# Sparse attention in a hybrid decoder layer: the top-k mask leaves the score products and is applied to the probabilities by VectorE

## The reference

```python
index = jnp.einsum('bqh,bqhs->bqs', iwb, jax.nn.relu(logits)) * idx_scale
index = jnp.where(causal[None], index.astype(jnp.float32), -jnp.inf)
_, sel = lax.top_k(index, topk)
...
s = jnp.einsum('bqhd,bqkd->bqhk', qb, kg) * scale
p = masked_softmax(s, valid)
return jnp.einsum('bqhk,bqkd->bqhd', p.astype(vg.dtype), vg)
```

## Time and profile before

| | |
|---|---|
| median of the runs | 3528.93 us (3526.89 to 3529.4) |
| profiled execution | 3532.62 us, of which span 3530.8 us |
| busy over the span | TensorE 96%, its weight loads 82%, VectorE 66%, ScalarE 51%, GpSimd 34% |
| mask products in D steps (L1737) | 272, of which 266 for tiles 2 to 15 |

### The profile page before, as it was taken

How to read it: one execution, slowest core, us unless ns; L and a number is a source line. 1 busy time by engine, 2 the same in 40 slices (tenths; PEclk the granted TensorE clock), 3 DMA queues, 4 the chain that set the end, 5 groups by cost and what they waited for, 6 DMA issues and landing times. The chain is left out here.

```text
span 3530.8 us, 55543 instructions
## 1 busy us (share of the span) xinstructions
PE 3376.6 (96%) x18952; PEld 2899.2 (82%) x18952; DVE 2319.4 (66%) x4885; ACT 1805.0 (51%) x3062; POOL 1190.9 (34%) x1963
## 2 busy tenths in 40 slices
PE   6999889899999999999999997999999999999998
PEld 6999777788888888888788785888888788888876
DVE  9899576667777777667743546765645666665364
ACT  4443356677877887886773333333323433333232
POOL 4343244554443333323220234332301435332031
PEclk9999999999999999999999998999999999999999
DMA  4345310000000000000010554322234532332444
GB/s 167 117 165 163 92 33 18 24 20 18 18 18 15 12 18 10 15 7 7 10 41 7 180 159 150 131 72 96 80 130 170 190 99 84 105 110 85 141 142 170
DMA packets 190051, 290.20 MB, mean 82 GB/s; under 512 B 33490, under 2 KB 130002, under 8 KB 189778
## 3 DMA queue, kind: packets, MB, share of 16 engines
q1 hardware_dynamic: 187700, 286.23, 24.5%
q10 hardware_dynamic: 2080, 0.52, 0.1%
HBM read 211.74 MB, written 74.97 MB: 81 GB/s over the span
## 5 line engine op out<-in xcount | busy, mean ns | idle before, releaser
L1849 ACT ACTIVATE shared<-a_ps_st 128x512 f32<-128x512 f32 x716 | 453.1, 637 | 262.3 <-PE a_ps_st L1737 154.3
L2982 PE MATMUL f_ps<-f_x_four,f_w_hi 128*128 128x512 f32 x1408 | 437.4, 392 | 11.8 <-DVE f_w_lo L3120 11.8
L2982 PE MATMUL f_ps<-f_x_three,f_w_hi 128*128 128x512 f32 x1056 | 325.5, 389 | 2.0 <-DVE f_w_lo L3120 2.0
L2982 PEld LDWEIGHTS f_ps<-f_x_four,f_w_hi 128*128 128x128 f32 x1408 | 266.1, 189 | 68.6 <-DVE f_w_lo L3120 13.3
L1761 PEld LDWEIGHTS a_ps_o<-a_vsl,shared 128*128 128x128 f32 x2176 | 289.1, 196 | 19.5
L1761 PEld LDWEIGHTS a_ps_o<-a_dv,shared 128*128 128x128 f32 x2176 | 282.2, 192 | 10.8
L1548 POOL TENSOR_SCALAR a_tk<-a_tk,a_halves 128x1 f32<-128x1 f32 x336 | 105.0, 312 | 539.6 <-ACT a_junk_a L1856 537.2
L1761 PE MATMUL a_ps_o<-a_vsl,shared 128*128 128x65 f32 x2176 | 280.5, 273 | 0.0
L2982 PE MATMUL f_ps<-f_x_four,f_w_lo 128*128 128x512 f32 x704 | 275.3, 391 | 0.0
L1761 PE MATMUL a_ps_o<-a_dv,shared 128*128 128x65 f32 x2176 | 273.8, 269 | 0.0
L3015 PE MATMUL f_ps<-f_w_hi 128*128 128x512 f32 x680 | 265.6, 391 | 4.9 <-DVE f_w_lo L3129 4.8
(11 more groups left out here) (405 smaller groups left out, 8816.9 us busy)
## 6 DMA issues: line engine op xcount, KB each, us to landing
shared<-in_w_down SPq DMA_DIRECT2D x88, 512.0 KB, 3.3
px_raw<-in_x_t SPq DMA_DIRECT2D x48, 512.0 KB, 4.6
shared<-in_w_gate SPq DMA_DIRECT2D x44, 512.0 KB, 5.0
shared<-in_w_up SPq DMA_DIRECT2D x44, 512.0 KB, 4.8
g_scratch<-shared SPq DMA_DIRECT2D x22, 1024.0 KB, 7.5
shared<-g_scratch SPq DMA_DIRECT2D x88, 256.0 KB, 3.5
z_scratch<-p_z SPq DMA_DIRECT2D x16, 768.0 KB, 5.2
o_scratch<-a_oacc SPq DMA_DIRECT2D x32, 256.0 KB, 2.1
```

The lines of the kernel that those rows point to most:

```text
L1849: act.activation(p_t[:, s % PT_RING, :], ps_st[s % ST_BANKS][:, :], ACT.Exp, scale=SCALE).then_inc(exp_done, 1)
L2982: mm = pe.matmul(out[:, :], w[:, j, k * P:(k + 1) * P], x_part(j, x)[:, k], start=(k == 0 and i == 0), stop=(k == 3 and i == 2))
```

## The change

For D quads of tiles 2 to 15 the mask product is no longer part of the score. Each mask is instead transposed once per tile by new side jobs "turn" (one per 512 keys: up to four products of a 128 x 128 piece of `mask_d` with the identity, on TensorE); ScalarE takes exp(0.125 x mask) of it into `keep_d`, which is 1 for a kept key and 0 for a masked one, in int8. After ScalarE's exponential of each D step, VectorE replaces p by min(1e30 x keep, p) in place ("keep" below), and the PV product waits for that. Planner constants change: a turn job costs 50, `MASK_TIME` is -300. The pick of the next mask waits for the last turn of the mask before (instead of the last D score). The scratch `junk_a` becomes int8, and two phases share a semaphore.

```diff
-SIDE_COST = {"max": 550, "cmax": 600, "idx": 680, "prep": 600, "aug": 150}
+SIDE_COST = {"turn": 50, "max": 550, "cmax": 600, "idx": 680, "prep": 600, "aug": 150}
-STEP_TIME, MASK_TIME, LEAST_ROOM = 1500, 0, 0.3
+STEP_TIME, MASK_TIME, LEAST_ROOM = 1500, -300, 0.3
...
+        for t in range(2, TILES):
+            for c in range(self.chunks[t]):
+                r = self.topk_due(t) + c
+                add(r, max(r + 1, self.first("D", t) - 2 * (self.chunks[t] - c)), SIDE_COST["turn"], ("turn", t, c))
...
+    d_steps = [s for s, (n, j) in enumerate(steps) if quads[n][0] == "D" and quads[n][1] >= 2]
+    d_no = {s: b for b, s in enumerate(d_steps)}
...
+        keep_d = sb("a_keep_d", [P, TILES, P], mybir.dt.int8)
-        junk_a = sb("a_junk_a", [P, SEQ], BF16)
+        junk_a = sb("a_junk_a", [P, SEQ], mybir.dt.int8)
...
+            def turn_mask(job):
+                _, t, c = job
+                if c == 0:
+                    pe.wait_ge(mask_d_done, mask_d_value(t))
+                out = side_bank(job)
+                w = min(CHUNK, (t + 1) * P - c * CHUNK)
+                for b in range(w // P):
+                    lo = c * CHUNK + b * P
+                    mm = pe.matmul(out[:, b * P:(b + 1) * P], mask_d[:, lo:lo + P], ident_b[:, :], start=(b == 0), stop=(b == w // P - 1), skip_group_check=True)
+                mm.then_inc(group_turned, 1)
...
-                    if kind == "D":
+                    if kind == "D" and i < 2:
                         pe.wait_ge(mask_d_done, mask_d_value(i))
...
-                    mask = mask_d[:, j * P:(j + 1) * P]
+                    mask = mask_d[:, j * P:(j + 1) * P] if i < 2 else None
...
+                if s in d_no:
+                    pe.wait_ge(kept, d_no[s] + 1)
...
+            def take_mask(job):
+                _, t, c = job
+                w = min(CHUNK, (t + 1) * P - c * CHUNK)
+                act.wait_ge(group_turned, turn_no[job] + 1)
+                if t >= 3 and c == 0:
+                    act.wait_ge(kept, d_no[plan.last[number[("D", t - 1, 1)]]] + 1)
+                dst = keep_d[:, 4 * c:4 * c + w // P, :].rearrange("p b q -> p (b q)")
+                act.activation(dst, ps_side[side_no[job] % SIDE_BANKS][:, 0:w], ACT.Exp, scale=SCALE).then_inc(evac_done, 1)
...
-                    dve.wait_ge(st_done, plan.after("D", t - 1))
+                    if t == 2:
+                        dve.wait_ge(st_done, plan.after("D", t - 1))
+                    else:
+                        dve.wait_ge(group_turned, turn_no[("turn", t - 1, plan.chunks[t - 1] - 1)] + 1)
...
+            def keep(s):
+                n, j = steps[s]
+                p = p_t[:, s % PT_RING, :].rearrange("p (h q) -> p h q", h=4)
+                dve.wait_ge(exp_done, s + 1)
+                if j == 0:
+                    dve.wait_ge(evac_done, evac_no[("turn", quads[n][1], plan.chunks[quads[n][1]] - 1)])
+                dve.scalar_tensor_tensor(p, keep_d[:, j, :].unsqueeze(1).broadcast_to([P, 4, P]), 1e30, p, ALU.mult, ALU.min).then_inc(kept, 1)
...
             for s in range(S + PV_LAG + 1):
+                if s - 1 in d_no:
+                    keep(s - 1)
...
-        fixed_set = sem("m_fixed_set")
+        fixed_set = mixer.fixed_set
...
-        fixed_set = sem("f_fixed_set")
+        fixed_set = mixer.fixed_set
...
-            pool.wait_ge(fixed_set, 3)
+            pool.wait_ge(fixed_set, 6)
```

More of the change, by code:

```diff
@@ L1339, in attention_phase @@
         exp_done = sem("a_exp_done")
+        kept = sem("a_kept")
         pv_done = sem("a_pv_done")
@@ L1771, in side @@
                     prep(job)
+                elif job[0] == "turn":
+                    turn_mask(job)
                 else:
@@ L1862, in evacuate @@
                     take_aug(job[1])
+                elif job[0] == "turn":
+                    take_mask(job)
                 elif job[0] == "idx":
@@ L2569, in __init__ @@
         self.x_lo_done = ctx.enter_context(nc.semaphore("f_x_lo_done"))
+        self.fixed_set = ctx.enter_context(nc.semaphore("f_fixed_set"))
     def part(self, j, low):
```

## The result

The changed kernel takes 3583.96 us (median of four executions, 3578.55 to 3597.02) beside 3528.55 us of the kernel before: a ratio of 1.0159 with a 95% interval of 1.0144 to 1.0174. It is 55 us slower. 3521 us had been predicted, with 3490 to 3556 as the range. The profiled execution took 3580.2 us with a span of 3578.4, so the trace has to explain 47.6 us of span.

A forecast was written before the change was run, and what follows sets the result against it. TensorE's queue was taken as the bound, ScalarE equally full in D g = 0 stages. Terms -13.3 - 3.2 + 0 + 12.5 - 26 + 9 + 13.3 = -7.7 us gave a 3521 us median, range 3490 to 3556.

The forecast's parts named there:

- I cost this at nothing on balance, with the two steps as cover: D steps: PV products waiting for keeps, and keeps for exponentials, cost 0 because VectorE may be two steps behind.
- Product, 0.23 us each: D steps from tile 2 on: 266 mask products leave TensorE at 0.23 us each, 61.2 us in all.
- Turns, 13.3 us: S stages: 133 mask blocks transposed on full TensorE at 0.10 us each cost 13.3 us; ScalarE's 41 evacuations count nothing.
- Keeps, 0.66 us each: VectorE in D steps: 266 added instructions at 0.66 us each, 175 us in all.
- g = 0, nothing, held by ScalarE: D(4..13), g = 0: ScalarE keeps its 189.8 us and VectorE rises to 189.0 of 192.2 us; gain 0.
- g = 1, +12.5 before the planner's part, about nothing with its 1.3 us a stage: D(4..13), g = 1: VectorE, at 226.8 us, exceeds the 202.3 us; 12.5 lost, planner giving back 1.3 a stage.
- The planner, -26 and +9: Side jobs leaving 20 D stages give back 26 us; the 40 or so jobs cost 9 us where TensorE is full.
- D(14), D(15), 13.3 us: Last four D stages, VectorE nearly free: 62 steps save TensorE 14.3 us, 1.0 lost to ScalarE in D(14); gain 13.3.
- Rival 2: VectorE becomes the D stages' bound, PV waits for keeps, moved jobs bring nothing: +26 us, 3555; chance 0.20.
- Rival 1: Full gain: VectorE absorbs the keeps in its idle time, 47.9 us saved, 3481; chance 0.12.
- Rival 3: GpSimd blocks VectorE's keeps: 42 us of VectorE, 21 on the path in g = 1; +13, 3542; chance 0.08.
- Rival 4: A turn stops TensorE, waiting for the last pick: 14 tiles at 1 us each, 3535; chance 0.07.

The follow-up runs named there:

- chain: The changed kernel with keeps cut to one element per partition, all waits standing; top-k mask left out of D probabilities: 3518.9 us, 0.9958.
- plan0: The changed kernel with MASK_TIME 0 instead of -300, so side jobs are spread as before the change: 3611.65 us, ratio 1.0213.
- load: The changed kernel with each keep replaced by a like instruction on a bf16 scratch tile, without the keep's waits; probabilities unmasked: 3564.45 us, 1.0085.
- nokeep: The changed kernel without keeps and without the PV product's wait for them; D probabilities unmasked: 3514.04 us, ratio 0.9938.
- bare: The kernel before with only the D mask product removed from tile 2 on; no turns or keeps, planner as before: 3519.83 us, ratio 0.9956.
- both: The changed kernel with the mask product left in the D scores as well; turns, keeps and MASK_TIME -300 stay: 3579.19 us, ratio 1.0127.

## Why the prediction was wrong

**The step that failed.** "I cost this at nothing on balance, with the two steps as cover": the new waits were priced apart from the load. Alone they do cost little (chain, 5 us). With the load they raise its cost from 51 to 78 us. The load's own cost failed too: the prediction booked +12.5 in g = 1 and nothing elsewhere, as if an engine could be filled to 98% (189.0 of 192.2) for free; in plan0, without the planner's shift, those g = 0 stages took 200.8 us, 8.6 more than before. The load run has VectorE busy 1183 of 1543 us, 77%, and loses 51 us against nokeep; 30.5 of them are in the g = 1 stages and the W stages behind them. "By the total it fits, by the stage it doesn't" was the right sentence, and the stages weren't counted to the end: W(5..14) g = 0 had VectorE busy 79.3 of 93.5 us already, and had to take late keeps and chores.

**The term that was missing.** Nothing in the sum says what TensorE's clock does once it waits. The row at hand, S(4) g = 0 with PE 10.72 of 15.4 us and clock 0.91, was read as a sign of a full VectorE and not as a price. The half clock went from 47.8 to 121.3 us. It answers in part where the gain of the removal went: in the g = 1 stages of bare, 95 products gave 2.5 us and 23.6 us of half clock, worth up to 11.8 of the 19.5 us that are missing. The Trainium skill (TensorE: Matmul & The Clock Gate, "What's actually happening") says that the clock follows how busy TensorE has lately been, with 1.2 and 2.4 GHz as its levels; this trace agrees as to the fall, D(5) g = 1 being at 0.50 after a stretch in which TensorE was busy 5.27 of 7.30 us. It doesn't show why the clock stays there for 20.5 us while TensorE's records cover all 20.00 us of the stage. In bare, work taken off TensorE in stages that something else half bounds did bring idle time and more half clock.

**By the prediction's own steps:**
- *Product, 0.23 us each*: right as a price where TensorE alone is the bound (0.23 in D(15)). As a sum of 61 us it failed: 14 us alone, 30 with the planner's shift, none with the keeps in.
- *Turns, 13.3 us*: 7 to 9, with ScalarE's evacuations in it. Of these the trace has 38, one for each turn job, not the 41 of the prediction.
- *Keeps, 0.66 us each*: somewhat high. The row of their line (min, median, longest in ns) is in the 0.66 to 0.75 foreseen for the records, but from start to start, with a maximum behind, a keep takes 0.60 to 0.61 us (862.48 to 863.09 in D(5)), so some 160 us in all, near the 158.7 of the window.

```profile
L2131 DVE SCALAR_TENSOR_TENSOR shared<-a_keep_d,shared x266: 668/689/1399, 598.4 to 1979.9; 128x512 f32<-128x512 int8 x133
```

- *g = 0, nothing, held by ScalarE*: right by bare (189.1 of 190.3 us). In the change it gained 2.9, because the planner had taken ScalarE's jobs out (173.6 instead of 189.8). That hid a cost: without keeps these stages take 177.7 us, so the keeps cost 11.6 us in them.
- *g = 1, +12.5 before the planner's part, about nothing with its 1.3 us a stage*: it lost 11.1 with it; without it (plan0) 58.3.
- *The planner, -26 and +9*: 17 in all; the shift is worth 22 with the keeps. The net held in size, though no run tests its two halves apart, so this is partly luck. Turns and moved jobs were priced at 22 us where TensorE is full; the S stages lost 16.0.
- *D(14), D(15), 13.3 us*: 7.6. D(15) kept its part; D(14) has ScalarE at 97% of its first half and a clock fall in the second.

**The rivals.** Rival 2 comes nearest: VectorE as the bound, PV waiting for the keep (16.8 us), the W stages crowded, though by late keeps and chores, not by moved jobs. It was priced at +26, against 47.6 of span; it too left out the clock and what a load short of full costs. Rival 1 fell with load. Rival 3, blocking by GpSimd, fell in the form it was given: the keeps average 0.715 us (190.1 us for 266), not above 0.9, and all that they take beyond their shortest is 12.5 us. It is seen, though, at a few: this keep beside a GpSimd copy took 1.18 us.

```profile
856.09 1.04 POOL L1483 CAST a_q_hi<-a_zd 128x1024 fp32r<-128x1024 f32 x1
...
856.50 1.18 DVE L2131 SCALAR_TENSOR_TENSOR shared<-a_keep_d,shared 128x512 f32<-128x512 int8 x1 [1.62 <-ACT shared L1881]
```

The rule of the Trainium skill (SBUF — State Buffer, "Who interferes with whom") that such a pair contends agrees with this row; what failed is my charge of 0.5 us for each overlap, the 42 us of rival 3.

The other side of it was not asked about, and the traces show something there. GpSimd's threshold instruction takes longer with the full keeps or their load, and not with keeps of one element. From the pages of nokeep, of the change and of load (chain has the 320 of nokeep):

```profile
L1557 POOL TENSOR_SCALAR a_tk<-a_tk,a_halves 128x1 f32<-128x1 f32 x336 | 107.5, 320 | 529.7 <-ACT a_junk_a L1889 527.6
...
L1556 POOL TENSOR_SCALAR a_tk<-a_tk,a_halves 128x1 f32<-128x1 f32 x336 | 127.7, 380 | 506.8 <-ACT a_junk_a L1888 504.7
...
L1558 POOL TENSOR_SCALAR a_tk<-a_tk,a_halves 128x1 f32<-128x1 f32 x336 | 130.0, 387 | 501.5 <-ACT a_junk_a L1888 499.2
```

ScalarE's counts wait for GpSimd's thresholds 51.5 us in the change, 39.5 in nokeep, and for VectorE's `a_halves` 21.1 against 14.8; the exponentials and Relus stand behind the counts in ScalarE's list. So a part of the load's cost may reach TensorE by way of GpSimd and ScalarE. The wait of 3.20 us ahead of the first clock fall went that way, but nothing shows that the keeps lengthened it, and no run separates this part.

Rival 4 fell: the turns cost 9 us at most.

**What stays open.** How the 47.6 us divide between VectorE's fullness and the clock: the clock's share is at most 36.8 us, but the two are coupled: both has 53 us less of it at a time 5 to 11 us lower, with 61 us more of TensorE work. How much of VectorE's load acts through GpSimd and ScalarE. And why load and waits together cost some 22 us more than apart, beyond the clock's part; moving the keep behind the maxima changed which wait TensorE meets and little of the time.

## What to carry to other kernels

Price a move from the bounding engine to another by stages, the ones behind the edit too, and count an engine as full from well below 100%: here a load of 77% over the whole, 94% in the g = 1 stages, cost 51 us. When work leaves TensorE in a stage that another engine partly bounds, the gain there can be next to nothing, as in bare, where waits and half clock took its place; look at the granted clock of each stage before crediting a saving. Where the receiving engine is really free, as in D(15), the start-to-start time of the removed instruction is what one gets: apply such a change there alone.

## What the runs showed of the hardware that was not expected

- With TensorE's mask products removed and nothing added (bare), D(14) g = 1 went from 24.8 to 30.1 us, at a mean granted clock of 0.77, 13.7 us of it at 1.2 GHz.
- At the half clock a score pass starts 0.53 us after the one before instead of 0.23, and eight PV products take 1.91 us instead of 1.00.
- With 61 us more of TensorE work (both), half clock fell from 121.3 to 68.3 us and the time did not rise.
- The same 336 GpSimd threshold instructions average 312 ns before, 320 with keeps of one element, 380 with the full keeps and 387 with the load alone.
